# V sums in two pairs of PSUM banks, and the scaled tokens in SBUF, in a PEER decoder layer

## The reference

```python
def block(xk):                       # 128 tokens
    q = (xk @ w_q).reshape(TOK_BLOCK, PEER_HEADS, 2, D_HALF)
    s = jnp.einsum('thpc,hpkc->thpk', q, sub_keys)
    ...                              # two top-16 lists, combined, top 16 of 256: eidx, top_s
    gate = jax.nn.softmax(top_s, axis=-1)
    u = u_tab[eidx]                  # 16 rows of 1024 for each token and head
    v = v_tab[eidx]
    h = jax.nn.gelu(jnp.einsum('td,thkd->thk', xk, u))
    coef = gate * h
    return jnp.einsum('thk,thkd->td', coef, v)
```

## Time and profile before

| | |
|---|---|
| median of 3 runs | 3044.41 us |
| the profiled execution | 3042.05 us |
| its span (first to last instruction) | 3040.2 us |
| PE, DVE, ACT, POOL busy | 57%, 71%, 30%, 68% |
| gathered by POOL's queue | 1107.43 MB, 304128 packets |
| granted TensorE clock, mean | 0.756 |

### The profile page before, as it was taken

How to read it: one execution, slowest core, us unless ns; L and a number is a source line. 1 busy time by engine, 2 the same in 40 slices (tenths; PEclk the granted TensorE clock), 3 DMA queues, 4 the chain that set the end, 5 groups by cost and what they waited for, 6 DMA issues and landing times.

```text
span 3040.2 us, 27752 instructions
## 1 busy us (share of the span) xinstructions
PE 1737.8 (57%) x7893; PEld 790.2 (26%) x7893; DVE 2156.3 (71%) x5259; ACT 919.1 (30%) x3125; POOL 2065.4 (68%) x2169
## 2 busy tenths in 40 slices
PE   8876667778567666666433333355536554335435
PEld 8853324434234233323100000011101111001102
DVE  8787877688676778888766556666677777666553
ACT  2334444243233322332222212333223332213302
POOL 2156676677676767667577777777777777777773
PEclk9988879889789788878665555677756777567668
DMA  6379999999999999999999999999999999999996
GB/s 184 106 270 402 400 409 395 356 398 406 402 409 402 409 404 402 403 404 402 400 406 406 408 406 406 391 409 409 410 410 408 407 405 409 402 409 408 403 410 256
DMA packets 370782, 1165.95 MB, mean 384 GB/s; under 512 B 35449, under 2 KB 96457, under 8 KB 370629
## 3 DMA queue, kind: packets, MB, share of 16 engines
q0 software_dynamic: 304128, 1107.43, 92.2%
q1 hardware_dynamic: 65968, 55.92, 5.8%
q10 hardware_dynamic: 533, 0.83, 0.1%
HBM read 1158.88 MB, written 5.15 MB: 383 GB/s over the span
## 4 chain that ended last, share of the span: by engine, by line
DMA 35%; POOL 23%; DVE 15%; issue 11%; PE 9%; ACT 1%; POOLq 0%; DVEq 0%; SPq 0%; ACTq 0%
DMA ex_v_row<-in_v_tab_dram,ex_v_idx 21%; POOL ex_v_row L1282 14%; DMA ex_u_row<-in_u_tab_dram,ex_eidx 10%; POOL ex_u_row L1282 9%; DVE ex_u_row L2029 6%; PE ex_acc L1921 6%; DMA ex_u_row<-in_u_tab_dram,m_first_idx 2%; PE ex_q L1818 1%; DMA m_wq<-in_w_in_dram 1%; DMA ex_v_row<-in_v_tab_dram,ex_few_idx 1%; DVE ex_same L1965 1%; DVE ex_same L1967 1%; DVE ex_idx L1968 1%; DVE ex_weight L2023 1%; DVE ex_best_at L1961 1%
## 5 line engine op out<-in xcount | busy, mean ns | idle before, releaser
L2029 DVE CUSTOM_DVE_ANT_0 ex_u_row<-ex_u_row,ex_xn 128x1024 f32<-128x1024 f32 x1056 | 1265.5, 1217 | 689.2 <-DMA ex_u_row<-in_u_tab_dram,ex_eidx 499.5
L1921 PE MATMUL ex_acc<-ex_v_row,ex_weight 128*32 128x512 f32 x4096 | 788.4, 909 | 1205.6 <-DMA ex_v_row<-in_v_tab_dram,ex_v_idx 1198.0
L1282 POOL DMA_INDIRECT ex_v_row<-in_v_tab_dram,ex_v_idx x1024 | 987.6, 964 | 428.4 <-issue 286.1
L1282 POOL DMA_INDIRECT ex_u_row<-in_u_tab_dram,ex_eidx x768 | 738.5, 962 | 262.7 <-issue 190.7
L1921 PEld LDWEIGHTS ex_acc<-ex_v_row,ex_weight 128*32 128x32 f32 x4096 | 157.9, 142 | 1692.7 <-issue 1683.7
L1282 POOL DMA_INDIRECT ex_u_row<-in_u_tab_dram,m_first_idx x256 | 246.9, 964 | 158.2 <-DVEq L2191 72.0
L1349 ACT COPY ex_spread_coef<-ex_coef 32x4 f32<-32x4 f32 x1024 | 195.7, 191 | 114.5 <-DVE ex_coef L2014 102.8
L1622 PE MATMUL ex_q<-m_mix,m_wq 128*128 128x384 f32 (+1 forms) x704 | 227.0, 477 | 0.0
L1512 ACT ACTIVATE ex_hact<-ex_hdot 128x16 f32<-128x16 f32 x66 | 14.2, 216 | 651.0 <-DVE ex_hdot L2029 650.7
L1622 PEld LDWEIGHTS ex_q<-m_mix,m_wq 128*128 128x128 f32 x704 | 136.6, 200 | 103.5 <-issue 41.6
L1338 ACT COPY ex_v_idx<-ex_eidx 32x4 uint32<-32x4 uint32 x768 | 146.0, 190 | 8.3
(11 more groups left out here) (438 smaller groups left out, 2315.6 us busy)
## 6 DMA issues: line engine op xcount, KB each, us to landing
ex_v_row<-in_v_tab_dram,ex_v_idx POOLq DMA_INDIRECT x1024
m_wq<-in_w_q_dram SPq DMA_DIRECT2D x14, 1024.0 KB, 17.3
ex_u_row<-in_u_tab_dram,ex_eidx POOLq DMA_INDIRECT x768, 12.8
fr_w<-in_w_in_dram SPq DMA_DIRECT2D x12, 512.0 KB, 4.9
ex_u_row<-in_u_tab_dram,m_first_idx POOLq DMA_INDIRECT x256, 12.7
m_wq<-in_w_in_dram SPq DMA_DIRECT2D x8, 512.0 KB, 21.4
m_mix<-in_w_ple_gate_dram SPq DMA_DIRECT2D x8, 512.0 KB, 16.6
out_y_prompt_dram<-m_wq SPq DMA_DIRECT2D x7, 512.0 KB, 6.4
```

The lines of the kernel that those rows point to most:

```text
L1282: pool.indirect_dma_start(out=row[:, :], out_offset=None, in_=table, in_offset=bass.IndirectOffsetOnAxis(ap=pick, axis=0)).then_inc(landed ...
L1921: last = nc.tensor.matmul(acc[g * TS:(g + 1) * TS, half, :], weight[:, b % 2, g * GROUPS + k // PACK, :], v_row[(n - PACK + 1 + g) % V_RIN ...
L2029: nc.vector.tensor_tensor_reduce(out=u_row[n % U_RING][:, :], in0=u_row[n % U_RING][:, :], in1=xn[:, :], scale=1.0, scalar=0.0, op0=ALU.mu ...
```

## The change

`acc` becomes a list of two pairs of banks, `sums`. Tile `t` uses `sums[t % 2]`, and the sample tokens the first pair. PE's wait at the start of tile `t` is now for `added >= t - 1`, from tile 2 on. To free two banks, `xn` becomes an SBUF tile. To free SBUF, the small tiles `few`, `few_expo` and `repeat` become views of `M.total` and `M.taps`.

```diff
-        few = ph.sb("few", [TS, 2, HEADS, TOPK])
-        few_expo, few_norm = ph.sb("few_expo", [TS, HEADS, TOPK]), ph.sb("few_norm", [TS, HEADS])
+        few = M.total[0:TS, 0:2 * P].rearrange("p (a h k) -> p a h k", a=2, h=HEADS)
+        few_expo, few_norm = M.total[0:TS, 2 * P:3 * P].rearrange("p (h k) -> p h k", h=HEADS), ph.sb("few_norm", [TS, HEADS])
...
-        repeat = ph.sb("repeat", [TS, P])
+        repeat = M.taps[0:TS].rearrange("p c k -> p (c k)")
...
-        acc = ph.ps("acc", [P, 2, HALF_D])
-        xn = ph.ps("xn", [P, D])
+        sums = [ph.ps(f"acc{r}", [P, 2, HALF_D]) for r in range(2)]
+        xn = ph.sb("xn", [P, D])
...
-        few_sums, few_gates = [[acc[q * TS:(q + 1) * TS, bank, 0:D // 4] for q in range(4)] for bank in range(2)]
+        few_sums, few_gates = [[sums[N_TILES % 2][q * TS:(q + 1) * TS, bank, 0:D // 4] for q in range(4)] for bank in range(2)]
...
-                    if h == 0 and k == 0 and t > 0:
+                    if h == 0 and k == 0 and t > 1:
 
-                        pe.wait_ge(added, t)
+                        pe.wait_ge(added, t - 1)
...
-                            last = nc.tensor.matmul(acc[g * TS:(g + 1) * TS, half, :], weight[:, b % 2, g * GROUPS + k // PACK, :],
+                            last = nc.tensor.matmul(sums[t % 2][g * TS:(g + 1) * TS, half, :], weight[:, b % 2, g * GROUPS + k // PACK, :],
...
-                nc.vector.tensor_tensor(kept(t), kept(t), acc[0:n, :, :].rearrange("p a (c e) -> p (a c) e", c=DC // 2), ALU.add).then_inc(added, 1)
+                nc.vector.tensor_tensor(kept(t), kept(t), sums[t % 2][0:n, :, :].rearrange("p a (c e) -> p (a c) e", c=DC // 2), ALU.add).then_inc(added, 1)
```

## The result

| | before | changed |
|---|---|---|
| median of 4 runs each | 3043.37 us (3042.01 to 3045.18) | 3217.11 us (3214.35 to 3219.51) |
| profiled execution (span) | 3042.05 (3040.2) | 3214.35 (3212.4) |

The ratio is 1.0565, 95% interval 1.0553 to 1.0578. The change costs 172 us between the two profiled executions.

The account below looks back on a forecast made before the run. Row transfers at 406 GB/s were taken to set the pace, with POOL's gather issue close behind; 3042 + 340 (held gathers) - 110 (slack) - 4 (bank pairs) = 3268, so 3270 us, range 3100 to 3430 us.

Parts of the forecast that it names:

- What bounds the kernel: Gathers at L1282: rows arrive one per 1.29 us at 406 GB/s, POOL's own minimum is 1.24 us per gather.
- Two SBUF inputs hold a gather: DVE operations with two SBUF inputs stretch POOL's gathers; a dot of 1.22 us holds POOL in its last 1.02 us.
- the first rival: Not slower: the dot takes nothing from POOL and gathers keep 0.94 us; 3038 us, chance 0.06.
- The size, 340 us: Time the 1056 dots add to POOL's gathers, taken a little above 213 to 290 us and below 458 us.
- The tally: Sum over 478 bursts of dots: 201 us first catches, 12 us followers, 0 to 76 us more; 213 to 290 us.
- the random formula: Gathers meeting the 1056 dots at random: 1056 x 0.42 = 444 us added to POOL's gathers.
- the second pattern: Dots starting every 1.14 us: POOL passes one, then is held 1.04 us by the next or slips in; 0 to 76 us.
- POOL's slack, 110 us of 160 taken back: Of POOL's 160 us of real waiting before gathers, two thirds, 110 us, offset the added time; ends 0 and 160.
- The pairs of banks, -4 us: PE no longer waits at a tile's start for the add of L2036 of the tile before; -4 us in all.
- A waiting gather waits for one operation only: With DVE operations back to back, a held gather is let go after one; read from four L2167 at 845.87.
- Rows stay the bound: Dots add only 143 us to POOL and its slack swallows it; 3042 to 3071 us, chance 0.08.
- The third rival: Random meeting and more: dots add 550 us to gathers, only 70 us taken back; 3518 us, chance 0.08.

Follow-up runs that it names:

- half dots: Dot over 512 instead of 1024 channels, in the changed kernel (ratio to before 0.9971 or 0.9964 with its control in the kernel before; medians 3324.33 and 3320.94 us).
- e1_xn_only: Changed kernel with xn in SBUF but the sums left in one pair of banks and the old wait; ratio to the kernel before 1.0196.
- f1_changed: The whole changed kernel run again, unaltered, on a chip where rows come at about 365 GB/s; 3363.15 us, ratio to the kernel before 1.0181.
- f3_dot_after_dot: Changed kernel with a DVE wait ahead of each dot for the dot before it; 3307.05 us, ratio to the kernel before 1.0003.

## Why the prediction was right

3270 us were forecast and 3217 came, 5.7% over before in place of 7.5%; the range of 3100 to 3430 held it. The mechanism was right, and one term of the sum, what POOL's waiting takes back, was too small. Step by step:

- **What bounds the kernel**: right. Transfers set the pace with POOL's floor close behind, and the changed kernel has POOL as its bound (chain 35% DMA before, 64% POOL after; the landing time halved).
- **Two SBUF inputs hold a gather, and the dot, a custom operation, is no exception**: right. A held gather ends 0.81 us after the dot. The half dots show that the hold goes with the dot's length, e1_xn_only that moving xn alone brings it. The rule of the Trainium skill (SBUF — State Buffer, Who interferes with whom) that such an instruction contends with a GpSimd instruction that reads SBUF agrees with the 694 stretched gathers. The inference in the same section of the Trainium skill that a `tensor_tensor` doesn't stall a DMA, which stood behind the first rival, does not hold for these gathers: L2023 before and L2029 after both hold them.
- **The size, 340 us**: 329 us measured. The tally gave 213 to 290 and the random formula 444; the choice between them was by judgement, and its good fit is partly luck: it was argued as "a held gather lands later and so breaks some of the neat bursts", and there are 542 bursts of dots after, 478 before. But the second pattern, a gather held for a whole dot, was sized too low: at most 76 us for 73 gathers, where the trace has 117 of 1.9 to 2.1 us, with 120 us held. And 13 gathers with 29 us are holds over several dots, which the prediction had ruled out.
- **POOL's slack, 110 us of 160 taken back**: this term was mis-sized. 156 us of 170 were taken back. (The 160 left out 17.6 us of waits before gathers for the sample tokens and for ACT, and took the pause as 0.30 in place of 0.304 us.) I had kept a third for waits behind a late ACT or DVE, taken as independent of POOL's pace. They weren't, in this trace: a slower POOL makes everything that it would wait for come in time (behind PE 135.6 to 12.1 us, behind the dots 100.0 to 1.1 us). With 156 in place of 110 and 329 in place of 340 the sum is 3042 + 329 - 156 - 4 = 3211 us, against 3214.35 measured. The forecast's whole excess is this term and 11 us of the other.
- **The pairs of banks, -4 us**: not contradicted, and never resolved. PE's wait of 13.4 us went as said; two measurements give 2 to 5 us, neither to be told from zero. What was bought with two banks was the removal of a wait that hardly ever held anything up.
- **"A waiting gather waits for one operation only"**: wrong. Four short L2167 had been read for it. Where a dot follows another with 61 to 63 ns of overlap, a gather can wait on, over up to seven dots (f1_changed). In the changed kernel 146 gathers were let go at the end of a dot that overlapped the next, 109 of them where the overlap was 72 to 77 ns, but one where it was 61. What decides between the two is not shown.
- **The rivals**: "the dot takes nothing" falls by the 694 held gathers. "Rows stay the bound" is wrong for the result's chip, where the tally's 143 us would have been needed, and half right where rows are slower: at 365 GB/s 294 us added to POOL cost 0.24%. The third rival's 550 us didn't come.
- **What would show it**: POOL's busy time in gathers rose by 329 us (340 said), its waits shrank to 14 us (60), the rate to 378 GB/s (370), one gather per 1.43 us (1.45), and DVE waits longer, 628.5 us for 499.5.

## What to carry to other kernels

Moving an operand of a long VectorE operation from PSUM to SBUF is not free when GpSimd issues indirect gathers beside it, even if that operation's own time stays the same (1220 and 1225 ns): look for the cost in the gathers' busy total and not in their median, and expect it to grow faster than the operation's length (here nearly with the square, from two lengths). Set against it the waiting of the engine that pays. In the result almost all of it was taken back (156 of 170 us), and the rest of the added time was paid in full; where rows were slower, a good 290 of some 430 us were taken back before time was lost. If such operations can't be avoided, try a short gap between them (here one wait for the operation before), which lets the gathers in and changes their step against the dots; at 365 GB/s it removed nearly the whole loss, at 406 GB/s it was not run.

## What the runs showed that was not expected

- A gather can be held over a whole train of back-to-back dots: 4.40 us over three, 9.09 us over seven. It always ends 0.81 or 0.82 us after the last. A gap of 0.14 us ends the hold.
- In f3_dot_after_dot seven gathers were caught each by a dot that started 0.20 us after it, later than the 0.13 us at which it reaches its point elsewhere. All seven stood behind the index search (L1946). Such a gather takes 2.2 us even with gaps. Why the dot catches it there is not shown.
- The same kernel gathers at 406 GB/s on the result's chip and at about 365 GB/s on four others, for a reason that no run shows. The same change costs 5.65% on the first and 1.8% on another (xn alone 1.9 and 2.0% on two): slower rows hide a slower issuer.
- One to four fulfilled waits ahead of a gather don't lengthen the 0.305 us pause between two of them.
